# Convolution tiles between the attention's steps, and chunk pairs in the recurrence, in a two-block fp32 transformer kernel

## The reference

```python
A = jnp.einsum('bhntd,bhnsd->bhnts', q_intra, k_intra)      # n: chunk, t, s: tokens in it
A = jnp.where(causal, A, 0.0)
o_intra = jnp.einsum('bhnts,bhnse->bhnte', A, v)
dS = jnp.einsum('bhnsd,bhnse->bhnde', k * jnp.exp(b_last - b), v)
S_next = dec[..., None] * S + ds
o = o_intra + einsum(q * jnp.exp(b), S_prev)
```

```python
proj = rms_norm_2(x, norm1_g) @ w_in + b_in                 # conv 2x1024, q 1024, k 128, v 128 columns
h = a * jax.nn.sigmoid(gate)                                # a, gate: halves of the conv columns
h = conv_depthwise(h, 31 taps, causal) + conv_dw_b
conv_out = silu(layer_norm(h, conv_ln_g, conv_ln_b))        # the norm runs over all 1024 channels
# attention: 16 q heads, 2 kv heads of 64; rms norm of q and k, rotary, band of 128, sinks, softmax
x = x + jnp.concatenate([conv_out, attn_out], -1) @ w_out
```

## Time and profile before

| what | us |
|---|---|
| median of 3 runs (3158.61 to 3161.42) | 3158.91 |
| the profiled execution | 3160.68 |
| its span, first to last instruction | 3158.9 |
| PE busy | 3068.7 |
| DVE busy | 1882.1 |
| ACT busy | 1628.0 |
| POOL busy | 668.6 |

### The profile page before, as it was taken

How to read it: one execution, slowest core, us unless ns; L and a number is a source line. 1 busy time by engine, 2 the same in 40 slices (tenths; PEclk the granted TensorE clock), 3 DMA queues, 4 the chain that set the end, 5 groups by cost and what they waited for, 6 DMA issues and landing times.

```text
span 3158.9 us, 63872 instructions
## 1 busy us (share of the span) xinstructions
PE 3068.7 (97%) x25380; PEld 2986.1 (95%) x25380; DVE 1882.1 (60%) x3274; ACT 1628.0 (52%) x2600; POOL 668.6 (21%) x292
## 2 busy tenths in 40 slices
PE   8999998999999999889999999999999999999999
PEld 8999998999999898768999999999999999999999
DVE  5555555744544458756677788644447865554444
ACT  5766665566687642375444443444444444444443
POOL 3333332444444333203434400000000000000000
PEclk9999998999999899999999999999999999999999
DMA  5443433444434354224445544455554455555554
GB/s 188 144 144 134 145 133 108 175 168 165 166 141 141 113 179 159 93 80 158 173 177 186 174 146 148 162 187 185 185 187 173 148 179 184 186 184 185 185 185 164
DMA packets 72286, 506.58 MB, mean 160 GB/s; under 512 B 7904, under 2 KB 10592, under 8 KB 11232
## 3 DMA queue, kind: packets, MB, share of 16 engines
q1 hardware_dynamic: 71584, 503.09, 46.1%
q10 hardware_dynamic: 576, 1.72, 0.2%
HBM read 502.69 MB, written 2.10 MB: 160 GB/s over the span
## 4 chain that ended last, share of the span: by engine, by line
PE 91%; DVE 5%; ACT 3%; issue 1%; DMA 0%; SPq 0%; DVEq 0%; ACTq 0%
PE bank L449 13%; PE bank L450 13%; PE bank L451 13%; PE bank L2170 4%; PE bank L2172 4%; PE banks L2172 4%; PE banks L2170 4%; PE bank L2171 4%; PE banks L2171 4%; PE bank L463 4%; PE banks L1965 3%; PE banks L1966 3%; PE banks L1967 3%; PE bank L1966 2%; PE bank L1965 2%; PE bank L1967 2%
## 5 line engine op out<-in xcount | busy, mean ns | idle before, releaser
L426 ACT ACTIVATE whi<-raw 128x1024 fp32r<-128x1024 f32 x898 | 943.4, 1059 | 1016.6 <-PE bank L451 420.6
L433 DVE TENSOR_TENSOR wlo<-raw,whi 128x1024 fp32r<-128x1024 f32 x667 | 812.6, 1229 | 466.5 <-ACT whi L426 465.5
L433 POOL TENSOR_TENSOR wlo<-raw,whi 128x1024 fp32r<-128x1024 f32 x231 | 608.0, 2633 | 1054.6 <-ACT whi L426 1054.6
L449 PE MATMUL bank<-xa_hi,whi 128*128 128x272 f32 (+1 forms) x2048 | 602.6, 294 | 3.0 <-DVE wlo L433 1.7
L450 PE MATMUL bank<-xa_lo,whi 128*128 128x272 f32 (+1 forms) x2048 | 592.9, 289 | 0.0
L451 PE MATMUL bank<-xa_hi,wlo 128*128 128x272 f32 (+1 forms) x2048 | 592.0, 289 | 0.0
L449 PEld LDWEIGHTS bank<-xa_hi,whi 128*128 128x128 f32 x2048 | 391.8, 191 | 7.4 <-issue 2.7
L450 PEld LDWEIGHTS bank<-xa_lo,whi 128*128 128x128 f32 x2048 | 391.8, 191 | 1.3
L451 PEld LDWEIGHTS bank<-xa_hi,wlo 128*128 128x128 f32 x2048 | 391.4, 191 | 0.0
L449 PE MATMUL bank<-xb_hi,whi 128*128 128x256 f32 (+1 forms) x1152 | 328.4, 285 | 0.1
L450 PE MATMUL bank<-xb_lo,whi 128*128 128x256 f32 (+1 forms) x1152 | 326.5, 283 | 0.0
(11 more groups left out here) (420 smaller groups left out, 6662.3 us busy)
## 6 DMA issues: line engine op xcount, KB each, us to landing
raw<-in_w SPq DMA_DIRECT2D x251, 1024.0 KB, 4.8
raw<-in_v SPq DMA_DIRECT2D x128, 1024.0 KB, 5.3
raw<-in_u SPq DMA_DIRECT2D x96, 1024.0 KB, 4.8
hT<-in_hT SPq DMA_DIRECT2D x4, 544.0 KB, 8.1
out<-hT SPq DMA_DIRECT2D x8, 256.0 KB, 2.3
r_keys<-in_keys ACTq DMA_DIRECT2D x1, 1024.0 KB, 4.8
c_mask<-in_masks ACTq DMA_DIRECT2D x1, 320.0 KB, 3.0
params<-in_params SPq DMA_DIRECT2D x1, 238.5 KB, 2.5
```

Of the source, the lines that this page charges most:

```text
L426: act.activation(whi[:, (2 * t.q + half) % 4, :], raw[:, t.q, half * 1024:(half + 1) * 1024], ACT.Copy).then_inc(w_hi_done, 1)
L433: eng.tensor_tensor(wlo[:, t.q, at], raw[:, t.q, at], whi[:, slot, :].bitcast(F32), ALU.subtract).then_inc(w_lo_done[half], 1)
L449: te.matmul(ps, hi, x[0][:, kk, cols], start=(kk == 0), stop=False)
```

## The change

In the recurrence, two chunks of 64 tokens form a block of 128: their scores are one 128x128 matmul, masked by a causal mask that is also zero between the two chunks, and their output is one matmul over 128 rows. Five score matmuls become three, and five output matmuls become three; the four state increments stay. The wait on `lower_rows` is for the small meta matmul, and one increment (rows 64 to 127) comes after it.

In the mixer, the weight tiles are reordered in memory. Four channel tiles of the convolution, then K and V, then the fifth channel tile and q0 stand before the rounds; the other three channel tiles stand in rounds 1 to 3, with the whole next q tile behind the scores. Rounds 4 to 8 are as before. The convolution's norm is spread over rounds 4 to 7, its products over rounds 7 and 8, and its splits over rounds 8 and 9. The w_out slices of round 8 begin with the attention's rows (slices 8 to 13), and `halves_done` counts both halves of such a tile at its last slice. The trigonometry of the rotary stands in front of the convolution. The unused tensor `gap` grows by 16 floats (64 bytes per partition), and everything declared after it moves by as much.

```diff
-            for c_ in range(NCH + 1):
-                cs, rows, _ = span(c_)
-                last = te.matmul(B_AT[rows, att_cols(c_)], g.ki[:, cs], g.qi[:, cs], start=True, stop=True)
-            last.then_inc(att_done, 1)
+            for n, cs in enumerate(tok):
+                te.matmul(B_AT[:, n * P:(n + 1) * P], g.ki[:, cs], g.qi[:, cs], start=True, stop=True)
+            te.matmul(B_AT[0:META, 2 * P:MASK_H], g.ki[:, 0:META], g.qi[:, 0:META], start=True, stop=True)\
+                .then_inc(att_done, 1)
...
-            for chs in ((0, 1, 3), (2, 4)):
-                for c_ in chs:
-                    cs, rows, n = span(c_)
-                    if c_ < NCH:
-                        ds = te.matmul(B_DS[:, c_ * P:(c_ + 1) * P], g.kst[rows, n, :], g.v[rows, n, :],
-                                       start=True, stop=True)
-                        if c_ == 2:
-                            ds.then_inc(ds_done, 1)
-                    last = te.matmul(B_O[:, cs], g.v[rows, n, :], g.att[rows, att_cols(c_)], start=(c_ == 0),
-                                     stop=False)
-                if chs[0] == 0:
-                    last.then_inc(lower_rows, 1)
-                    te.wait_ge(lower_rows, h)
+            for c_ in (0, 1, 3, 2):
+                cs, rows, n = span(c_)
+                if c_ == 2:
+                    te.matmul(B_O[:, 0:META], g.v[0:META, 2, :], g.att[0:META, 2 * P:MASK_H], start=True,
+                              stop=False).then_inc(lower_rows, 1)
+                    for m, cols in enumerate(tok):
+                        te.matmul(B_O[:, cols], g.v[:, m, :], g.att[:, m * P:(m + 1) * P], start=False, stop=False)
+                    te.wait_ge(lower_rows, h)
+                ds = te.matmul(B_DS[:, c_ * P:(c_ + 1) * P], g.kst[rows, n, :], g.v[rows, n, :],
+                               start=True, stop=True)
+            ds.then_inc(ds_done, 1)
...
-        tensor(ctx, "gap", [P, P])
+        tensor(ctx, "gap", [P, P + 16])
...
+CONV_AT = (0, 2, 4, 6, 10, 13, 16, 19)
+T_SWK = T_CONV + 8
+Q_AT = (12, 15, 18, 21, 22, 23, 24, 25)
...
+        CONV_MUL_AT = {7: (0, 2), 8: (4, 6)}
+        CONV_SPLIT_AT = {8: (0, 2), 9: (4, 6)}
+        IN_PRELUDE = 5
+        FREE = CONV_T - IN_PRELUDE + 1
...
+            te.wait_ge(xn1_done, KT)                       # swa_tensor
+            for k in range(IN_PRELUDE - 1):
+                project_conv(k, 0)
+                project_conv(k, 1)
             project_fp32(te, Tile(T_SWK, 0, 0), xn1, SEQ)
+            project_fp32(te, Tile(T_SWV, 0, 0), xn1, SEQ)
+            project_conv(IN_PRELUDE - 1, 0, range(0, 8))
             te.wait_ge(S.k_bias, 1)
             te.matmul(PS_SUM, ..., c.ksq[:], start=True, stop=True).then_inc(S.k_sum, 1)
             te.wait_ge(S.v_bias, 1)
             ...                                            # transposes of v
+            project_conv(IN_PRELUDE - 1, 0, range(8, 16))
+            project_conv(IN_PRELUDE - 1, 1, range(0, 8))
             te.wait_ge(S.k_n, 1)
             te.matmul(PS_ROT, ..., c.kn[:], start=True, stop=True).then_inc(S.k_rot, 1)
+            project_conv(IN_PRELUDE - 1, 1, range(8, 16))
+            project_q(0, range(KT))
             for s in range(1, NQ + 1):
+                s < FREE: conv a | sum | conv gate 0:8 | transposes, rot | conv gate 8:16 | scores, out | q tile s
+                s == FREE: conv_sums at the end;  s == FREE + 1: conv_squares at the end
+                s == NQ: w_out slices (0,8)(0,10) | (0,12)(1,8) | (1,10)(1,12) | (0,0)(0,2)(1,0)(1,2)
+            swa_transposes(te, NQ - 1); slices (0,4)(0,6); swa_out(te, NQ - 1); slices (1,4)(1,6)
...
+                if s <= FREE:                              # swa_vector, before the scaling of q
+                    conv_steps(ve, k - 1, False)
+                if s < FREE:
+                    conv_evac_a(ve, k)
+                if s == FREE + 1:
+                    ve.wait_ge(S.mean, 1)                  # centring
...
+                if s < FREE:                               # after the row maxima
+                    conv_steps(ve, k, True)
+                if s == FREE + 2:
+                    ve.wait_ge(S.rstd, 1)                  # scaling
+                if s in CONV_MUL_AT:                       # products with the sigmoid
...
+                    if s == FREE + 2:                      # swa_scalar, before q_root
+                        act.wait_ge(S.var, 1)              # Ln, Exp of the variance
...
+                if s == FREE + 1:                          # after the copy of the transposes: squares
+                if s == FREE + 3:                          # eight sigmoids
```

More of the change, by code:

```diff
@@ L451, in project @@
                     last = te.matmul(ps, lo, x[0][:, kk, cols], start=False, stop=(kk == KT - 1))
-                last.then_inc(halves_done, counts[half])
+                last.then_inc(halves_done, 1)
         RESUMED = (T_WOUT, T_WOUT + 1)
@@ L498, in body @@
                     if base == T_WOUT and static(i) and 4 * i + s < 2:
[L499 removed]
+                        wout_piece(te, s, KT - 2)
                     else:
@@ L1418, in wout_piece, with conv_sums @@
                 te.matmul(ps, hi, xa[1][:, kk, 0:SEQ], start=False, stop=False)
-                last = te.matmul(ps, lo, xa[0][:, kk, 0:SEQ], start=False, stop=False)
-            if tile == 0 and k0 == 6:
-                last.then_inc(halves_done, 1)
+                last = te.matmul(ps, lo, xa[0][:, kk, 0:SEQ], start=False, stop=(kk == KT - 1))
+            if k0 == KT - 2:
+                last.then_inc(halves_done, 2)
+        def conv_sums(te):
+            te.wait_ge(cv_done, CONV_T)
+            for k in range(CONV_T):
+                last = te.matmul(PS_MEAN, con("ones"), c.cv[:, k, :], start=(k == 0), stop=(k == CONV_T - 1))
+            last.then_inc(S.mean, 1)
@@ L1423, in swa_tensor, with conv_squares, project_conv, wout_pieces @@
+        def conv_squares(te):
+            for m in range(2):
+                te.wait_ge(S.csq, m + 1)
+                for k in range(4 * m, 4 * m + 4):
+                    last = te.matmul(PS_VAR, con("ones"), c.side[:, k, :], start=(k == 0), stop=(k == CONV_T - 1))
+            last.then_inc(S.var, 1)
         def swa_tensor(te, ch):
             def project_q(j, pieces):
-                if j < NQ:
-                    project_fp32(te, q_tile(j), xn1, SEQ, pieces)
+                project_fp32(te, q_tile(j), xn1, SEQ, pieces)
+            def project_conv(k, gate, pieces=range(KT)):
+                project_fp32(te, conv_tile(k, gate), xn1, SEQ, pieces)
+            def wout_pieces(*which):
+                for tile, k0 in which:
+                    wout_piece(te, tile, k0)
+            te.wait_ge(xn1_done, KT)
+            for k in range(IN_PRELUDE - 1):
+                project_conv(k, 0)
+                project_conv(k, 1)
@@ L1434, in swa_tensor @@
-            te.wait_ge(S.k_n, 1)
-            te.matmul(PS_ROT, c.mask[:, MASK_S:MASK_S + P], c.kn[:], start=True, stop=True).then_inc(S.k_rot, 1)
             te.wait_ge(S.v_bias, 1)
@@ L1459, in swa_tensor @@
                 swa_rot(te, s - 1)
-                if s < NQ:
+                if s < FREE:
+                    project_conv(k, 1, range(8, 16))
+                elif s < NQ:
                     project_q(s, range(8, 12))
                 else:
-                    wout_piece(te, 1, 0)
-                    wout_piece(te, 1, 2)
-                if s == 1:
-                    for m in range(2):
-                        te.wait_ge(S.csq, m + 1)
-                        for k in range(4 * m, 4 * m + 4):
-                            last = te.matmul(PS_VAR, con("ones"), c.side[:, k, :], start=(k == 0),
-                                             stop=(k == CONV_T - 1))
-                    last.then_inc(S.var, 1)
+                    wout_pieces((1, 10), (1, 12))
                 swa_scores(te, s - 1)
@@ L1490, in swa_scalar @@
             act.activation(c.cos[:], c.half[:], ACT.Sin).then_inc(S.table, 1)
+            for k in range(IN_PRELUDE - 1):
+                conv_gate(act, k)
+                side_products(act, k + 1)
             act.wait_ge(evacuated, T_SWK + 1)
@@ L1675, in swa_pool @@
         def swa_pool(po, ch):
-            side_sum(po, CONV_T)
+            for k in range(CONV_T):
+                side_sum(po, k + 1)
             for tile in range(2):
@@ L2388 @@
              for x in (pq[2 * h], u[4 * h], pq[2 * h + 1], u[4 * h + 1], u[4 * h + 2], u[4 * h + 3])]
+    ct, kvt2, qt = interleave(tiles(w2[:, :C]), tiles(w2[:, C:2 * C])), tiles(w2[:, 3 * C:]), tiles(q_w)
+    at = {**{x + i: ct[2 * k + i] for k, x in enumerate(CONV_AT) for i in range(2)},
+          **{T_SWK - T_CONV + i: kvt2[i] for i in range(2)}, **{x: qt[j] for j, x in enumerate(Q_AT)}}
+    mixer = [at[i] for i in range(NATIVE)]
     w_all = np.concatenate([
```

279 lines of the change are left out of this document (124 added, 155 removed).

## The result

The changed kernel takes 3129.17 us (median of 4 runs, 3126.73 to 3130.61) against 3158.76 (4 runs, 3157.28 to 3161.42): ratio 0.9905, 95% interval 0.989 to 0.992. That is 29.6 us faster, twice the 15 forecast and outside the range of 3134 to 3156. The profiled execution took 3130.61 us, its span 3128.8.

What follows compares the result with a forecast made beforehand. PE, busy 3068.7 of 3158.9 us, was taken as the bound, so only its waits, lower clock or surplus work could yield time. Mixer -8, recurrence -7 and 64 bytes 0 made -15: 3144 us, range 3134 to 3156.

Steps and rivals of the forecast that it cites:

- The 64 bytes: Growth of the unused tensor gap, moving whi, hT, xb, xa and all behind them; taken as 0, ends -2 and +3.
- The recurrence: 16 heads: output and state from 2.51 to 2.05 us a head, scores unchanged; 7 us saved, ends nothing and 11.
- the recurrence gains nothing, changes of row group cost 0.2 us each: Rival: row group changes use up the recurrence's saving, leaving -8 in all, 3151 us; chance 0.12.
- The mixer: Same PE work, only order and waits move; stage from 277.1 to 269 us, gain 8, ends 15 and 0.
- round 4, c_qn: Last ten taps, 8.5 us with POOL beside them, stand before c_qn: stall 6.3 us, called the largest.
- round 7, c_q and c_qn: Mixer: POOL's split and the scaling stand before q6's copy; stalls 3.6 + 1.3 us.
- before round 8, c_q: Sigmoids, split halves and exps on ACT, first convolution products on DVE before q7: stall 6.3 to 8, 6.5 taken.
- the 5 for the clock: Mixer stage: half-speed spells behind four stalls of 3.5 us or more, about 1.3 each; 5 us.
- Both better, 3135 to 3139: Rival: mixer rounds 4 to 8 at the upper end, 11 us in the recurrence; -24; chance 0.16.
- The stage only moves its stalls: Rival: mixer stalls 6.3 in round 4, 6.5 in round 8; only the recurrence gains; -7, 3152 us; chance 0.13.
- Slower: the norm is too late: Rival: norm's chain queues with the last five attention rounds, stalls 10 us in rounds 7 and 8; 3167; chance 0.08.
- The rotation's 0.3 us is short: Rival: the rotation's slack in mixer rounds 1 to 3 fails, each round stalls 2 us; 3150 us; chance 0.05.

Runs made afterwards that it cites:

- e1: The kernel before with the 64 bytes in gap alone; 3145.95 us, ratio 0.9963.
- e4: The changed kernel without the 64 bytes, so both the recurrence and the mixer change at the old placement; 3144.51 us, ratio 0.9952.
- e2: The kernel before with the recurrence's chunk pairs alone, old placement; 3153.57 us, ratio 0.9985.
- e3: The kernel before with the mixer change alone, old placement and old recurrence; 3148.52 us, ratio 0.9963.
- e5: The kernel before with 64 bytes ahead of whi and 64 more behind it; 3157.21 us, ratio 0.9989.
- e6: The kernel before with 64 bytes behind whi only, so only the moving operands move; 3159.35 us, ratio 0.9991.
- e7: The kernel before with 128 bytes in the gap in place of 64; 3163.69 us, ratio 1.001.
- e13: The kernel before with only raw (the low weights) moved, so that whi stands 160 bytes past it modulo 256; 3150.90 us, ratio 0.9976.
- e15: The kernel before with whi and all behind it moved by 32 bytes, distance 128 from raw; 3178.89 us, ratio 1.0068.
- e16: The kernel before with whi and all behind it moved by 96 bytes, distance 192 from raw; 3155.02 us, ratio 0.9985.
- e8: The changed kernel with pads that put raw and e_coef_hi at multiples of 256 bytes as well; 3161.01 us, ratio 1.0006.
- e14: The changed kernel with raw, whi and all behind whi moved together by 64 bytes, distance still 160; 3139.11 us, ratio 0.9942.

## Why the prediction was wrong, step by step

**The 64 bytes: the step that failed.** The prediction put them at 0, with ends of -2 and +3, since "PE rows on xa, xb and e_coef, at different places, have one pace". They were worth -12.1 alone (e1) and about -15 on top of the rest (3129.17 against e4's 3144.51). The evidence was read too coarsely: the paces before were 355.0, 354.8 and 353.3, and a difference of 1.7 ns over a few thousand triples is several us. The reason was weak too: tensors at different places that run at one pace would not have shown that other places have it. The forecast named this outcome as a way to be wrong ("rows of unchanged work at another pace") but gave it no price.

**The recurrence: forecast -7, measured -4.5 by time and -6.7 (e2) to -8.2 by profile, but for another reason: the size was right by luck.** Weight loads of one head, for the earlier trace rows:

```profile
264.64 0.53 PEld L678 LDWEIGHTS banks<-g_qi,g_ki 128*128 128x128 f32 x4
265.29 0.11 PEld L679 LDWEIGHTS banks<-g_qi,g_ki 128*16 128x16 f32 x2
265.43 0.30 PEld L683 LDWEIGHTS bank<-g_osq,consts 128*128 128x128 f32 x2
...
272.10 0.93 PEld L701 LDWEIGHTS banks<-g_v,g_kst 16*128 16x128 f32 x6 [0.15 <-issue]
273.15 0.29 PEld L695 LDWEIGHTS banks<-g_att,g_v 16*128 16x128 f32 x2
273.47 0.52 PEld L698 LDWEIGHTS banks<-g_att,g_v 128*128 128x128 f32 x4
274.11 0.29 PEld L701 LDWEIGHTS banks<-g_v,g_kst 64*128 64x128 f32 x2
274.53 0.19 PEld L450 LDWEIGHTS bank<-xa_hi,whi 128*128 128x128 f32 x1
```

From 272.10 to 274.53 are 2.43 us, not the 2.05 forecast (the earlier trace rows had 2.51), and the scores take 0.79 (264.64 to 265.43), where the forecast was 0.54; before they took 0.53 and the 0.22 of idle ahead of them. Over the 15 heads in which they stand between projections, the scores, outputs and increments, with the transposes ahead of the scores and the sum behind them, took 57.0 us from start to start before and 56.7 after: next to nothing was gained in them. The 7 us are in the projections behind them, in the clock. PE's windows over the same two stretches, before and then after:

```profile
260.00:360.00 100.00, 99.83 (x779) 0.97 0.40 137
360.00:460.00 100.00, 99.77 (x774) 0.97 0.40 137
```

```profile
260.00:360.00 100.00, 100.00 (x777) 1.00 0.42 145
360.00:460.00 100.00, 100.00 (x773) 1.00 0.42 139
```

And where a head ends, in the kernel before (the last 64-row matmuls start at 276.39), then in the changed kernel:

```profile
273.00:276.80 3.80, 3.74 (x29) 1.00 0.26 67
276.90:280.00 3.10, 3.10 (x14) 0.51 0.59 246
280.50:283.50 3.00, 3.00 (x26) 1.00 0.00 0
```

```profile
271.00:274.50 3.50, 3.50 (x24) 1.00 0.33 61
274.60:277.60 3.00, 3.00 (x24) 1.00 0.61 257
```

After some heads the granted clock falls to 1.2 GHz (0.51) for 3.4 us. The nine profiles with the old recurrence have 5, 4, 6, 3, 9, 4, 4, 4 and 7 such spells (before, e1, e3, e5, e6, e7, e13, e15, e16) between 60 us and the recurrence's last head, the eleven with the new one none. (All twenty have one long spell of 20 to 24 us at the very end of the recurrence; it is no part of this.) A line through the nine puts the recurrence's end at 518.8 us plus 1.7 us for each spell, so 8 us for the five in the profile before; the eleven without spells end between 518.4 and 522.8. The number differs by execution and is a good part of the scatter of the old kernel's times (3151 to 3165). Whether the 64-row matmuls or the wait of 0.20 us between them bring a spell on was not tried; the change takes away four of the seven 64-row matmuls of a head, and the wait. The rival "the recurrence gains nothing, changes of row group cost 0.2 us each" was right on the matmuls and wrong on the time.

**The mixer: forecast -8, measured -9.7 (e3) to -10.7.** Its sum stands, term by term, but for two:

```
                       forecast  measured
bias of V, prelude        3.0      2.5
rounds 1 to 3             none     none
round 4, c_qn             6.3      4.7, and 0.9 on c_pr
round 5 and round 6       1.05+2.0 0.4+1.9, and 1.2 on c_qf
round 7, c_q and c_qn     3.6+1.3  0.9+1.0
before round 8, c_q       6.5      7.1
round 8, c_qn             1.0      none
c_pr behind the products  2.7      2.1
last split xa_lo          2.1      2.3
wlo of tile 2             1.8      1.85
stage                     269      266.4
```

The 1.05 of round 5 is the idle time of the clean round that the prediction built on. Round 4's wait is 1.6 us shorter since the last ten taps took 4.03 us (1338.55 to 1342.58) and not 8.5: POOL's sum, which was to stretch them, had ended at 1338.28 and stretched only small operations ahead of them. Round 7 is off by 3.0 us since POOL's split fell on the rotary of round 6 and not on the copy of q6: that operation took 2.31 us (L1688), beside 0.43 elsewhere, and makes the 1.2 on `c_qf`. The waits add up to 26.8 us where the forecast had 31.4, and the rest of the stage is 239.6 where it had 237.6, the 5 for the clock among them. Half clock: 1335 to 1355 ran at a granted 0.83, behind the 4.7 us wait, and 1400 to 1433 at 0.79, behind the 7.1 us one. The term of 5 us for it can't be read off by itself; as the rest of the stage came out 2 us above its sum, it may have been somewhat small.

The wait before round 8 was 7.1 us, between the 6.5 taken and the 8 that came with a full hold by POOL's split. The two scalings that took 3.37 us end at 1403.53, when POOL's split does (4.73 us from 1398.65); they were held only for the part that was left of it. The rule that the prediction took from the Trainium skill, "SBUF — State Buffer", section "Who interferes with whom", is on instructions with two SBUF inputs. These two have one, so they are no case of it; L1688 in round 6 has two and agrees, since it began at 1379.33 inside the first half of POOL's split (from 1379.00, 4.84 us for two halves) and took 2.31 us.

**The rivals.** "Both better, 3135 to 3139" came closest to the time, by the wrong road: both stages gained as in the main forecast, and the third part, the 64 bytes, brought the rest. "The stage only moves its stalls" is excluded by the stage's -9.7 to -10.7. "Slower: the norm is too late" didn't come: the stalls in rounds 7 and 8 stayed under the 10 us from which it was to decide. "The rotation's 0.3 us is short" is excluded by the three rounds without a wait.

## What to carry to other kernels

An edit that moves buffers is an edit of every matmul that reads them: price it, or time the kernel with the move alone first. Where PE is busy all the time, count its matmuls per 200 us at full clock before and after, in stages whose code is the same; a span that shrinks under "PE 100% busy" is pace, not order. A group of small matmuls can cost nearly the same before and after a change and still differ in the clock of the work behind it (2.51 against 2.43 us here, but 3.4 us at 1.2 GHz behind some of the old ones), so look at PEclk in windows around them before counting their cycles.

## What the runs showed of the hardware that was not expected

- The pace of three fp32r matmuls of 256 columns, each with its weight load, lay between 346.7 and 360.0 ns at full clock by nothing but where the weights' halves and the moving operands start: 4% on TensorE. In the whole kernel with the same work in the same order, that is 32 us between e15 (3178.89) and e1 (3145.95), and 31 us between e8 (3161.01) and the changed kernel (3129.17), each against its own before. Seen modulo 256, the weights' distances 160 and 192 were the good ones when `whi` moved with the moving operand, 128 the worst. For the down product, `e_coef_hi` at the same place as `e_coef_lo` was bad each time (357.1 to 360.0), and 160 past it was little better (355.6 to 357.3 in e5, e7 and e14). What in the chip does this is open.
- Within one projection stage the triples of single slices lie between 350.0 and 361.1 ns (kernel before), in an order that goes with the start of the moving slice: 64 bytes more on that tensor shift the order by one slice.
- With one placement the down product runs at 348.9, 353.3 or 355.6 ns for a whole segment, by execution: so one profile doesn't price a placement to better than 7 us a segment (1024 triples by 6.7 ns).
- A stretch of 64-row fp32 matmuls with PE busy 98% (3.74 of 3.80 us) was followed in a third of the heads (46 spells in nine profiles of 15 heads) by 3.4 us at 1.2 GHz.
